# A hybrid decoder block with 32 experts: weights of the first pair loaded by halves, weights of the last pair by units of 4 MB

## The chip, the cores and the metric

The kernel runs on one core of one Trainium2 chip. The metric is the device time of the kernel in microseconds. The time before is the median of three runs, 1120.93 us (1120.08 to 1121.37). All arithmetic on weights is in float32 or in pairs of a rounded high part and a low part.

## The reference

One layer of a decoder for 256 tokens of width 1024: a normalization, one projection of 5632 columns, an attention with 8 heads, a gated recurrence with 4 heads, and their merging by sigmoid gates; then, with `x` the residual stream,

```python
x = x + mixed @ w_out[l]                      # 1024 x 1024
h2 = rmsnorm(x, norm2_w[l])
logits = h2 @ router_w                        # 32 experts
top_v, top_e = lax.top_k(logits, 4)           # softmax over the four
gu = xb @ w_gate_up[e] + b_gate_up[e]         # 1024 x 2048 for each expert
glu = gate * sigmoid(1.702 * gate)            # gate, up clamped at 7
y = ((up + 1.0) * glu) @ w_down[e] + b_down[e]  # 1024 x 1024
x = x + (sum of the four weighted y)
```

and a last normalization. All 32 experts are computed, so 32 x 12 MB of expert weights are read from HBM.

## The kernel before

**The expert weights.** Experts are taken in pairs, 16 in all. The weights of a pair are 24 MB in 12 slots of 2 MB (128 partitions of 16 KB): slots 0 to 3 are gate/up of the pair's first expert, 4 to 7 those of the second, 8 and 9 the output weights (`w_down`) of the first, 10 and 11 those of the second. Two neighbouring slots are a unit of 4 MB. The ring in SBUF has just 12 slots (`slots`), so slot m of the next pair is loaded over slot m of this one once TensorE has used it. All these loads are issued by SyncE, in order, on one DMA queue. `load` (L475) loads a slot, `load_unit` (L479) a unit in one DMA. `load_pair` (L543) issues a pair's loads: where `by_slots` (L443) holds, each slot waits for its own release (`used`, L534) and is a DMA of its own; elsewhere both slots of a unit are waited for and one DMA of 4 MB follows. Before, `by_slots` holds for pairs 0, 1 and the last one (15). Slots 10 and 11 of the last pair are loaded in five parts (`parts`, L567, issued at L572): 1, 1, 1, 0.5 and 0.5 MB, each with a semaphore.

**What TensorE does with a pair.** `pair` runs gate/up of the first expert (slots 0 to 3, 16 matmuls a slot, L1817), then `combine` of the pair before (L1785), transpositions of the activation (`act_T`, L1863), gate/up of the second expert (slots 4 to 7), the output matmuls of the first (slots 8, 9, L1880), the gathering for the next pair (L1765) and the output matmuls of the second (slots 10, 11). In the last pair, the combinations of pair 14 lie between its slots instead, and a transposition of the second expert's activation lies between slots 8 and 9. After the last slot the result is combined once more (L1976), normalized and stored. Before each slot `arrived` (L1790) waits: for an even slot on `slot_loaded[m]`, for an odd one only if it was loaded on its own.

**Before the experts.** The dense weights come through a ring of three raw buffers. ScalarE rounds a piece of a weight to its high part (`round_hi`, L677) in a buffer `hi_a` to `hi_d`, and VectorE puts the low part over the raw data (`form_lo`, L464). `PIECES` (L38 on) says which half of which weight goes into which buffer. `hu`, `wo0` and `wo1` are the recurrence's up-projection and the two column halves of `w_out`. The slots of pair 0 lie over these buffers: slot 4 over the low parts of `hu`, 11 over its high parts (`hi_d`), 3 and 5 over high (`hi_a`) and low parts of `wo0`, 6 and 10 over those of `wo1`. So they can be loaded only once the matmuls that read them are through.

`mixed` (L1630) computes `wo0` for both token tiles (256 tokens are two tiles of 128). The high parts of `wo0` lie as two blocks of 256 columns with all 8 chunks of rows each, so every matmul reads both blocks, and both are needed until the end:

```python
for tt in range(TT):            # chunks 0 to 3: high, rest
turn_mix(3)
for tt in range(TT):            # chunks 4 to 7: high, rest
for tt in range(TT):            # chunks 0 to 7: low part of the input; end(...)
```

`wo1` is already handled in two halves of rows (chunks 0 to 3, 4 to 7), and `half_used` (L1732) marks that the first is done with.

SyncE issues the loads of pair 0 that lie over `hu`, `wo0` and `wo1` in this order: when `hu3` is full, slots 4 and 11; when `wo10` (the second tile of `wo0`) is full, slots 3 and 5; on `half_used`, the first halves of 6 and 10; when `wo11` is full, their second halves; last slot 9. Then pair 1 follows, its slot 0 in two halves (L550, L552).

Of the kernel before, what the change touches and what calls it, by code (L numbers as in the profile page):

```python
# [11 lines left out]
P = 128  # L12
# [3 lines left out]
KD = D // P  # L16
# [13 lines left out]
PAIRS = E // 2  # L30
# [23 lines left out]
    [(GA1, j, "dve", ("D", j), "kT1") for j in range(2)] + [(GB0, j, "dve", ("A", j), "ga1") for j in range(2)] + \  # L54
    [(GB1, j, "dve", ("D", j), "ga3") for j in range(2)] + \
    [("mu", j, "dve", ("QA", j), "gb1") for j in range(4)] + [("hu", j, "dve", ("QD", j), "gb3") for j in range(4)] + \
    [("wo0", j, "dve", ("A", j), "mu3") for j in range(2)] + [("wo1", j, "dve", ("KB", j), None) for j in range(2)]
AT_PIECE = {(p[0], p[1]): n for n, p in enumerate(PIECES)}


# [66 lines left out]
def hybrid_block(nc, A, out):  # L127
    ctx = ExitStack()
    with ctx:
# [186 lines left out]
        def hi_part(where):  # L316

            buf, j = where
            if buf == "KB":
                return hi_b[:, 2048 * j:2048 * j + 2048].rearrange("p (k n) -> p k n", k=4)  # L320
            if buf in ("QA", "QD"):
                return {"QA": hi_a, "QD": hi_d}[buf][:, 1024 * j:1024 * j + 1024].rearrange("p (k n) -> p k n", k=4)
            return {"A": hi_a, "B": hi_b, "C": hi_c, "D": hi_d}[buf][:, 2048 * j:2048 * j + 2048].rearrange(
                "p (k n) -> p k n", k=KD)
# [10 lines left out]
        def raw_part(what, j, lo=False):  # L335

            s, kn = LOADS.index(what) % RING, 4 if what in ("mu", "hu") else KD
            whole = w_lo[s].rearrange("p (k n) -> p k n", k=kn) if lo else (wr4 if kn == 4 else wr8)[s]
            return whole[:, 4 * j:4 * j + 4, :] if what == "wo1" else whole[:, :, 256 * j:256 * j + 256]


        PS = [ctx.enter_context(nc.psum_tensor(f"PS{b}", [P, 512], F32)) for b in range(BANKS)]
# [46 lines left out]
        first_loaded, cst_loaded, router_loaded = sem("first_loaded"), sem("cst_loaded"), sem("router_loaded")  # L389

        first_half_used = sem("first_half_used")
        x_free, half_used, half_loaded = sem("x_free"), sem("half_used"), sem("half_loaded")

        slot_loaded = [sem(f"slot_loaded{m}") for m in range(12)]
        part_loaded = [sem(f"part_loaded{n}") for n in range(3)]
# [46 lines left out]

        def by_slots(j, m, first_round):  # L443

            return not first_round or j < 2 or j == PAIRS - 1

        def odd_loads(m, first_round, pairs=PAIRS):

# [22 lines left out]
        def _(sp):  # L471
# [41 lines left out]
                    sp.dma_start(MSK, A["lmask"].rearrange("p (m t) -> p m t", t=CHUNK)).then_inc(lmask_loaded, 16)  # L513


            filled(sp, "hu3")
            load(0, 0, 4)
            load(0, 0, 11)
            filled(sp, "wo10")
            for m in (3, 5):  # L520
                load(0, 0, m)
            for part in range(2):
                if part:
                    filled(sp, "wo11")
                else:
                    sp.wait_ge(half_used, 1)
                c = slice(2048 * part, 2048 * part + 2048)
                for m in (6, 10):
                    sp.dma_start(slots(m)[:, c], slot_src(0, m)[:, c]).then_inc(slot_loaded[m] if part else half_loaded, 16)
            filled(sp, "lg1")  # L530
            sp.wait_ge(root2_ready, TT)
            load(0, 0, 9)
# [10 lines left out]
            def load_pair(p, e, j, first_round, stop=12):  # L543

                for m in range(0, stop, 2):
                    if by_slots(j, m, first_round):
                        for n in (m, m + 1):
                            if first_round and j == 1 and n == 0:
                                sp.wait_ge(first_half_used, 1)
                                sp.dma_start(slots(0)[:, 0:2048], slot_src(e, 0)[:, 0:2048]).then_inc(half_loaded, 16)  # L550
                                used(0, 0)
                                sp.dma_start(slots(0)[:, 2048:], slot_src(e, 0)[:, 2048:4096]).then_inc(slot_loaded[0], 16)  # L552
                                continue
                            used(p + (n - SLOTS) // 12, (n - SLOTS) % 12)
                            load(e, j, n)
                    else:
                        for n in (m, m + 1):
                            used(p + (n - SLOTS) // 12, (n - SLOTS) % 12)
                        load_unit(e, j, m)
# [826 lines left out]
        def _(pe):  # L1386
# [243 lines left out]
            def mixed():  # L1630

                ps = [claim("wo00"), claim("wo10")]
                n, s = AT_PIECE["wo0", 1], LOADS.index("wo0") % RING
                w_h = hi_a.rearrange("p (j k n) -> p k j n", j=2, k=KD)
                w_l = w_lo[s].rearrange("p (k n) -> p k n", k=KD)

                def high(tt, ks):
                    for k in ks:
                        mm(ps[tt][:].rearrange("p (j n) -> p j n", j=2), mix_hi[:, k, P * tt:P * tt + P], w_h[:, k],
                           start=(k == 0), stop=False)  # L1640

                def rest(tt, ks):
                    for k in ks:
                        mm(ps[tt][:], mix_hi[:, k, P * tt:P * tt + P], w_l[:, k, :], start=False, stop=False)

                pe.wait_ge(hi_ready, n + 1)
                for tt in range(TT):
                    pe.wait_ge(mix_hi_ready, tt + 1)
                    high(tt, range(4))
                    wait_lo("wo0", 1)  # L1650
                    rest(tt, range(4))
                turn_mix(3)
                for tt in range(TT):
                    pe.wait_ge(mix_hi_ready, tt + 3)
                    high(tt, range(4, 8))
                    rest(tt, range(4, 8))
                for tt in range(TT):
                    wait_drained(pe, f"mT{2 + tt}")
                    for k in range(KD):
                        ins = mm(ps[tt][:].rearrange("p (j n) -> p j n", j=2), mix_lo[k // 4][:, k % 4, P * tt:P * tt + P], w_h[:, k],  # L1660
                                 start=False, stop=(k == KD - 1))
                    end(ins, f"wo{tt}0")

            mixed()
            def keep_clock(free_bank, cols):
# [63 lines left out]
            claim("wo11")  # L1729
            high1(ps[1], 1, 0)  # L1730
            rest1(ps[1], 1, 0)
            low1(ps[1], 1, 0).then_inc(half_used, 1)  # L1732
            high1(ps[0], 0, 1)
            rest1(ps[0], 0, 1)
            end(low1(ps[0], 0, 1), "wo01")
# [54 lines left out]
            def arrived(at, m):  # L1790

                r, j = at
                slot = ring(j, m)
                if isinstance(r, int) and isinstance(j, int) and j == 0 and m in (6, 10):
                    pe.wait_ge(half_loaded, 32)
                if not isinstance(j, int) and m == 0:
                    pe.wait_ge(half_loaded, 48)
                if m % 2 == 0:
                    pe.wait_ge(slot_loaded[m], 16 * (j + 1) if isinstance(r, int) else r * (16 * PAIRS) + 16 * (j + 1))
                elif not isinstance(j, int):  # L1800
                    pe.wait_ge(slot_loaded[m], 32)
                elif isinstance(r, int):
                    if by_slots(j, m - 1, True):
                        pe.wait_ge(slot_loaded[m], 16 * odd_loads(m, True, j + 1))
                else:
                    pe.wait_ge(slot_loaded[m], r * (16 * PAIRS) + 16 * (odd_loads(m, True) - PAIRS + j + 1))
                return slot
# [219 lines left out]
```

## Time and profile before

| what | us |
| --- | --- |
| median of 3 runs | 1120.93 |
| the profiled execution, its own time | 1120.51 |
| its span, first to last instruction | 1118.7 |
| TensorE busy | 1081.1 (97%) |
| VectorE, ScalarE, GpSimd busy | 347.6, 223.1, 47.9 |
| DMA | 438.77 MB, 392 GB/s over the span |

The time lies some 1.8 us over the span. Times in the views are counted from the start of the span. In a timeline, a row merges neighbouring instructions of one kind: start, duration of the whole, engine (PE is TensorE, DVE VectorE, ACT ScalarE, SPq SyncE's queue), line, operation, tiles (output<-inputs) and count; brackets tell how long the engine stood still before and on what it waited. `M`, `W`, `PS` are the names of the buffers; all slots are parts of `W`.

### The profile page before, as it was taken

Reading aid. Unit: us, or ns where it says so; the run is one execution under the profiler, and the core shown is the slowest. Engines: PE = TensorE matmul, PEld = TensorE weight load, DVE = VectorE, ACT = ScalarE, POOL = GpSimd, SP = SyncE. Lnnn points to the kernel's source line nnn. Section 1 sums busy time; section 2 is a strip of 40 time slices with the busy share of each in tenths; the row PEclk is TensorE's granted clock in tenths of the full one; section 3 lists DMA queues with packets and bytes.
Section 4 is the critical chain, followed back from the end, with each engine's and each line's share of the span. In section 5 each row is a group of like instructions: output and inputs, shape, how many; then the busy total and the mean of one; then the engine's idle time right before and its main releaser. Section 6 shows DMA issues by size and latency. Waiting matters only on the chain.

```text
span 1118.7 us, 14793 instructions
## 1 busy us (share of the span) xinstructions
PE 1081.1 (97%) x6265; PEld 528.2 (47%) x6265; DVE 347.6 (31%) x685; ACT 223.1 (20%) x355; POOL 47.9 (4%) x38
## 2 busy tenths in 40 slices
PE   7999999999999999999999999899999999999997
PEld 7889888734343434343443434234343334343432
DVE  4994888422222130312222221030303030312212
ACT  6645774301010101010101010001010101010102
POOL 0392000000000000000000000000000000000000
PEclk9999999999999999999999999899999999999999
DMA  9547549999999999999999999999999999999996
GB/s 323 194 152 308 218 163 388 382 425 400 418 431 432 431 431 431 431 432 431 431 431 431 431 431 431 431 431 431 432 431 435 434 431 431 431 435 431 422 426 247
DMA packets 35625, 438.77 MB, mean 392 GB/s; under 512 B 2900, under 2 KB 5736, under 8 KB 20488
## 3 DMA queue, kind: packets, MB, share of 16 engines
q1 hardware_dynamic: 34672, 437.76, 93.2%
q10 hardware_dynamic: 920, 0.56, 0.2%
q8 instruction: 23, 0.38, 0.1%
q14 instruction: 10, 0.08, 0.0%
HBM read 437.25 MB, written 1.05 MB: 392 GB/s over the span
## 4 chain that ended last, share of the span: by engine, by line
PE 71%; DMA 17%; DVE 2%; issue 1%; another core or an unknown queue 1%; SPq 0%; ACT 0%; DVEq 0%
PE PS L1817 31%; PE PS L1880 16%; DMA W<-in_w_gate_up_dram 9%; DMA W<-in_w_down_dram 8%; PE PS L1765 4%; PE PS L1785 4%; PE PS L1863 2%; PE PS L1469 2%; PE PS L1473 2%; PE PS L1476 2%; PE PS L1839 1%; PE PS L1455 1%; PE PS L1900 1%; DVE w_lo L464 1%
## 5 line engine op out<-in xcount | busy, mean ns | idle before, releaser
L1817 PE MATMUL PS<-W,M 128*64 128x512 f32 x2048 | 458.0, 599 | 16.0 <-DMA W<-in_w_gate_up_dram 10.2
L1817 PEld LDWEIGHTS PS<-W,M 128*64 128x64 f32 x2048 | 142.6, 138 | 300.1 <-issue 280.8
L1880 PE MATMUL PS<-W,M 128*64 128x512 f32 x1024 | 226.5, 594 | 7.7 <-DMA W<-in_w_down_dram 7.6
L1288 DVE TENSOR_SCALAR M<-PS 128x256 f32<-128x256 f32 x64 | 27.0, 422 | 512.2 <-PE PS L1817 512.2
L1880 PEld LDWEIGHTS PS<-W,M 128*64 128x64 f32 x1024 | 73.7, 137 | 146.1 <-issue 141.4
L868 ACT ACTIVATE M<-M 128x256 f32<-128x256 f32 x64 | 26.7, 417 | 474.3 <-DVE M L1288 474.3
L873 ACT COPY M<-PS 64x512 f32<-64x512 f32 x31 | 17.9, 578 | 268.8 <-PE PS L1880 268.8
L1304 DVE COPY M<-PS 128x512 f32<-128x512 f32 x32 | 22.1, 691 | 131.6 <-PE PS L1863 131.6
L1765 PE MATMUL PS<-M,X 128*128 128x128 f32 x480 | 57.6, 278 | 0.0
L1785 PE MATMUL PS<-M,SELT 128*128 128x512 f32 x120 | 55.8, 606 | 0.0
L1765 PEld LDWEIGHTS PS<-M,X 128*128 128x128 f32 x480 | 54.7, 192 | 1.0
L638 POOL TENSOR_SCALAR W<-W,SMALL 128x512 f32<-128x512 f32 x1 | 1.9, 1854 | 1010.9 <-DVE SMALL L1371 1010.9
L1298 DVE TENSOR_TENSOR M<-M 128x256 f32<-128x256 f32 x64 | 38.6, 604 | 4.9 <-ACT M L868 2.7
L1785 PEld LDWEIGHTS PS<-M,SELT 128*128 128x128 f32 x120 | 21.5, 189 | 34.0 <-issue 34.0
L1863 PE MATMUL PS<-CST,M 64*64 64x64 f32 x1024 | 36.7, 221 | 0.0
L464 DVE TENSOR_TENSOR w_lo<-raw,hi_a 128x2048 fp32r<-128x2048 f32 (+1 forms) x16 | 32.5, 2054 | 11.3 <-ACT hi_a L677 11.3
L1863 PEld LDWEIGHTS PS<-CST,M 64*64 64x64 f32 x1024 | 32.3, 134 | 5.9 <-issue 2.4
L1280 DVE TENSOR_TENSOR M<-PS,SMALL 128x512 f32<-128x512 f32 x32 | 22.1, 692 | 33.9 <-PE PS L1765 32.6
L1473 PE MATMUL PS<-w_lo,hT_hi 128*128 128x512 f32 x128 | 31.7, 389 | 0.0
L1294 DVE SCALAR_TENSOR_TENSOR M<-M 128x256 f32<-128x256 f32 x64 | 27.2, 425 | 2.2
L677 ACT CAST hi_a<-raw 128x2048 fp32r<-128x2048 f32 (+1 forms) x16 | 26.6, 1694 | 4.3 <-DMA raw<-in_w_in_dram 2.6
L1292 DVE TENSOR_SCALAR M<-PS 128x256 f32<-128x256 f32 x64 | 26.4, 413 | 0.0
(267 smaller groups left out, 853.5 us busy)
## 6 DMA issues: line engine op xcount, KB each, us to landing
W<-in_w_gate_up_dram SPq DMA_DIRECT2D x52, 4096.0 KB, 41.3
W<-in_w_down_dram SPq DMA_DIRECT2D x26, 4096.0 KB, 44.0
W<-in_w_gate_up_dram SPq DMA_DIRECT2D x22, 2048.0 KB, 12.6
raw<-in_w_in_dram SPq DMA_DIRECT2D x10, 2048.0 KB, 8.7
W<-in_w_down_dram SPq DMA_DIRECT2D x9, 2048.0 KB, 12.7
W<-in_w_down_dram SPq DMA_DIRECT2D x5, 1024.0 KB, 45.8
raw<-in_w_out_dram SPq DMA_DIRECT2D x2, 2048.0 KB, 10.5
W<-in_w_gate_up_dram SPq DMA_DIRECT2D x4, 1024.0 KB, 8.0
```

What stands on the lines that cost most here:

```text
L464: tensor_tensor(raw_part(what, j, lo=True), raw_part(what, j), hi_part(PIECES[n][3]), ALU.subtract).then_inc(lo_ready[PIECES[n][2]], 1)
L677: st.did(nc.scalar.copy(hi_part(PIECES[n][3]), raw_part(what, j)), hi_ready)
L868: nc.scalar.activation(sg, gate[b], ACT.Sigmoid, scale=ALPHA).then_inc(sigm_ready, 1)
L1288: v.tensor_scalar(gate[b], g2[:, :, 0], LIMIT, None, ALU.min).then_inc(gate_ready, 1)
L1294: v.scalar_tensor_tensor(out=up[b], in0=up[b], scalar=1.0, in1=gate[b], op0=ALU.add, op1=ALU.mult).then_inc(up_ready, 1)
L1298: v.tensor_tensor(act[b].rearrange("p (c q) -> p q c", c=8)[:, 32 * half:32 * half + 32, :], up[b].rearrange("p (q c) -> p q c", c=8), sg. ...
L1473: mm(ps[:], hi[:, k, rows], w_l[:, k], start=False, stop=False)
L1765: ins = mm(dst[:, P * a:P * a + P], hidden(tt, 4 * part + a), sel[:, tt, :], start=(tt == 0), stop=(tt == TT - 1))
L1785: ins = mm(acc[tt][n][:], selT[:, P * tt:P * tt + P], Y[:, 512 * n:512 * n + 512], start=False, stop=True, skip_group_check=True)
L1817: ins = mm(gu[half][64 * g:64 * g + 64, :], hTe[:, k, tok], gu_slot[slot][:, kk, c:c + 512], start=(k == 0), stop=(k == KD - 1))
L1863: ins = mm((gu[1] if b else multi)[rows, cols], act[b][rows, cols], ident[rows, rows], start=True, stop=True)
L1880: ins = mm(dst[64 * n:64 * n + 64, :], actT[b][:, 4 * kh + k, :], dn_slot[slot][:, k, 512 * n:512 * n + 512], start=(kh == 0 and k == 0), ...
```

## The change

Five things change. `wo0`'s high parts are laid out by halves of rows in `hi_a` (piece name `KA`), and `mixed` goes through it by halves of rows. The first half of `wo0` gets a mark of its own (`half_used["wo0"]`). The first loads of slots 4, 11, 3 and 5 are issued by halves, each half as soon as its part of the buffer is free: `hu1`, `hu3`, `half_used["wo0"]`, `wo10`. Slot 4's halves are column halves, the others contiguous halves of a partition's row. In `arrived`, the six slots of pair 0 that come in halves wait for all six first halves together; the first half of slot 0 of pair 1 has a semaphore of its own. And in the last pair `by_slots` holds from slot 10 on only, so that its slots 0 to 9 come as five units of 4 MB.

```diff
@@ -54,7 +54,7 @@
     [(GA1, j, "dve", ("D", j), "kT1") for j in range(2)] + [(GB0, j, "dve", ("A", j), "ga1") for j in range(2)] + \
     [(GB1, j, "dve", ("D", j), "ga3") for j in range(2)] + \
     [("mu", j, "dve", ("QA", j), "gb1") for j in range(4)] + [("hu", j, "dve", ("QD", j), "gb3") for j in range(4)] + \
-    [("wo0", j, "dve", ("A", j), "mu3") for j in range(2)] + [("wo1", j, "dve", ("KB", j), None) for j in range(2)]
+    [("wo0", j, "dve", ("KA", j), "mu3") for j in range(2)] + [("wo1", j, "dve", ("KB", j), None) for j in range(2)]
 AT_PIECE = {(p[0], p[1]): n for n, p in enumerate(PIECES)}
 
 
@@ -316,8 +316,8 @@
         def hi_part(where):
 
             buf, j = where
-            if buf == "KB":
-                return hi_b[:, 2048 * j:2048 * j + 2048].rearrange("p (k n) -> p k n", k=4)
+            if buf in ("KA", "KB"):
+                return (hi_a if buf == "KA" else hi_b)[:, 2048 * j:2048 * j + 2048].rearrange("p (k n) -> p k n", k=4)
             if buf in ("QA", "QD"):
                 return {"QA": hi_a, "QD": hi_d}[buf][:, 1024 * j:1024 * j + 1024].rearrange("p (k n) -> p k n", k=4)
             return {"A": hi_a, "B": hi_b, "C": hi_c, "D": hi_d}[buf][:, 2048 * j:2048 * j + 2048].rearrange(
@@ -336,7 +336,7 @@
 
             s, kn = LOADS.index(what) % RING, 4 if what in ("mu", "hu") else KD
             whole = w_lo[s].rearrange("p (k n) -> p k n", k=kn) if lo else (wr4 if kn == 4 else wr8)[s]
-            return whole[:, 4 * j:4 * j + 4, :] if what == "wo1" else whole[:, :, 256 * j:256 * j + 256]
+            return whole[:, 4 * j:4 * j + 4, :] if what in ("wo0", "wo1") else whole[:, :, 256 * j:256 * j + 256]
 
 
         PS = [ctx.enter_context(nc.psum_tensor(f"PS{b}", [P, 512], F32)) for b in range(BANKS)]
@@ -442,7 +443,7 @@
 
         def by_slots(j, m, first_round):
 
-            return not first_round or j < 2 or j == PAIRS - 1
+            return not first_round or j < 2 or (j == PAIRS - 1 and m >= 10)
 
         def odd_loads(m, first_round, pairs=PAIRS):
 
@@ -513,20 +514,26 @@
                     sp.dma_start(MSK, A["lmask"].rearrange("p (m t) -> p m t", t=CHUNK)).then_inc(lmask_loaded, 16)
 
 
-            filled(sp, "hu3")
-            load(0, 0, 4)
-            load(0, 0, 11)
-            filled(sp, "wo10")
-            for m in (3, 5):
-                load(0, 0, m)
+            def load_half(m, part, across=False):
+
+                to, src = slots(m), slot_src(0, m)
+                if across:
+                    to, src = (a.rearrange("p (k n) -> p k n", k=4)[:, :, 512 * part:512 * part + 512] for a in (to, src))
+                else:
+                    to, src = (a[:, 2048 * part:2048 * part + 2048] for a in (to, src))
+                sp.dma_start(to, src).then_inc(slot_loaded[m] if part else half_loaded, 16)
+
             for part in range(2):
-                if part:
-                    filled(sp, "wo11")
-                else:
-                    sp.wait_ge(half_used, 1)
-                c = slice(2048 * part, 2048 * part + 2048)
-                for m in (6, 10):
-                    sp.dma_start(slots(m)[:, c], slot_src(0, m)[:, c]).then_inc(slot_loaded[m] if part else half_loaded, 16)
+                filled(sp, f"hu{2 * part + 1}")
+                load_half(4, part, across=True)
+                load_half(11, part)
+            for what, pair_of in (("wo0", (3, 5)), ("wo1", (6, 10))):
+                sp.wait_ge(half_used[what], 1)
+                for m in pair_of:
+                    load_half(m, 0)
+                filled(sp, "wo10" if what == "wo0" else "wo11")
+                for m in pair_of:
+                    load_half(m, 1)
             filled(sp, "lg1")
             sp.wait_ge(root2_ready, TT)
             load(0, 0, 9)
@@ -1630,36 +1637,36 @@
             def mixed():
 
                 ps = [claim("wo00"), claim("wo10")]
-                n, s = AT_PIECE["wo0", 1], LOADS.index("wo0") % RING
-                w_h = hi_a.rearrange("p (j k n) -> p k j n", j=2, k=KD)
-                w_l = w_lo[s].rearrange("p (k n) -> p k n", k=KD)
-
-                def high(tt, ks):
+                w_h = hi_a.rearrange("p (k n) -> p k n", k=KD)
+                w_l = w_lo[LOADS.index("wo0") % RING].rearrange("p (k n) -> p k n", k=KD)
+
+                def high_and_rest(tt, kh):
+                    pe.wait_ge(mix_hi_ready, 2 * kh + tt + 1)
+                    ks = range(4 * kh, 4 * kh + 4)
                     for k in ks:
-                        mm(ps[tt][:].rearrange("p (j n) -> p j n", j=2), mix_hi[:, k, P * tt:P * tt + P], w_h[:, k],
-                           start=(k == 0), stop=False)
-
-                def rest(tt, ks):
+                        mm(ps[tt][:], mix_hi[:, k, P * tt:P * tt + P], w_h[:, k], start=(k == 0), stop=False)
+                    wait_lo("wo0", kh)
                     for k in ks:
-                        mm(ps[tt][:], mix_hi[:, k, P * tt:P * tt + P], w_l[:, k, :], start=False, stop=False)
-
-                pe.wait_ge(hi_ready, n + 1)
+                        mm(ps[tt][:], mix_hi[:, k, P * tt:P * tt + P], w_l[:, k], start=False, stop=False)
+
+                def low(tt, kh):
+                    wait_drained(pe, f"mT{2 * kh + tt}")
+                    for k in range(4):
+                        ins = mm(ps[tt][:], mix_lo[kh][:, k, P * tt:P * tt + P], w_h[:, 4 * kh + k],
+                                 start=False, stop=(kh == 1 and k == 3))
+                    return ins
+
+                pe.wait_ge(hi_ready, AT_PIECE["wo0", 0] + 1)
                 for tt in range(TT):
-                    pe.wait_ge(mix_hi_ready, tt + 1)
-                    high(tt, range(4))
-                    wait_lo("wo0", 1)
-                    rest(tt, range(4))
+                    high_and_rest(tt, 0)
                 turn_mix(3)
+                low(0, 0)
+                low(1, 0).then_inc(half_used["wo0"], 1)
+                pe.wait_ge(hi_ready, AT_PIECE["wo0", 1] + 1)
                 for tt in range(TT):
-                    pe.wait_ge(mix_hi_ready, tt + 3)
-                    high(tt, range(4, 8))
-                    rest(tt, range(4, 8))
+                    high_and_rest(tt, 1)
                 for tt in range(TT):
-                    wait_drained(pe, f"mT{2 + tt}")
-                    for k in range(KD):
-                        ins = mm(ps[tt][:].rearrange("p (j n) -> p j n", j=2), mix_lo[k // 4][:, k % 4, P * tt:P * tt + P], w_h[:, k],
-                                 start=False, stop=(k == KD - 1))
-                    end(ins, f"wo{tt}0")
+                    end(low(tt, 1), f"wo{tt}0")
 
             mixed()
             def keep_clock(free_bank, cols):
@@ -1729,7 +1736,7 @@
             claim("wo11")
             high1(ps[1], 1, 0)
             rest1(ps[1], 1, 0)
-            low1(ps[1], 1, 0).then_inc(half_used, 1)
+            low1(ps[1], 1, 0).then_inc(half_used["wo1"], 1)
             high1(ps[0], 0, 1)
             rest1(ps[0], 0, 1)
             end(low1(ps[0], 0, 1), "wo01")
@@ -1791,10 +1798,10 @@
 
                 r, j = at
                 slot = ring(j, m)
-                if isinstance(r, int) and isinstance(j, int) and j == 0 and m in (6, 10):
-                    pe.wait_ge(half_loaded, 32)
+                if isinstance(r, int) and isinstance(j, int) and j == 0 and m in (3, 4, 5, 6, 10, 11):
+                    pe.wait_ge(half_loaded, 6 * 16)
                 if not isinstance(j, int) and m == 0:
-                    pe.wait_ge(half_loaded, 48)
+                    pe.wait_ge(first_half_loaded, 16)
                 if m % 2 == 0:
                     pe.wait_ge(slot_loaded[m], 16 * (j + 1) if isinstance(r, int) else r * (16 * PAIRS) + 16 * (j + 1))
                 elif not isinstance(j, int):
```

Beside it, the declarations of the semaphores are changed, and slot 0 of pair 1 counts on `first_half_loaded`.

## Rows read from the trace of the kernel before

**Rows 1.** The page: its head, and TensorE in part 1.

```profile
span 1118.7 us, 14793 instructions
...
PE 1081.1 (97%) x6265; PEld 528.2 (47%) x6265; DVE 347.6 (31%) x685; ACT 223.1 (20%) x355; POOL 47.9 (4%) x38
```

**Rows 2.** Busy time by stretches; last three columns: TensorE's clock, DMA share, GB/s.

```profile
183.00:224.00 41.00, 40.39 (x222) 31.42 (x222) 22.64 (x53) 13.67 (x25) 0.00 (x0) 1.00 0.93 373
...
300.00:660.00 360.00, 358.74 (x2045) 145.91 (x2043) 75.14 (x186) 38.28 (x67) 0.00 (x0) 1.00 1.00 431
660.00:1046.00 386.00, 366.80 (x2031) 146.38 (x2028) 78.73 (x200) 37.05 (x67) 0.00 (x0) 0.99 1.00 431
```

**Rows 3.** Timeline of TensorE, 891 to 1040 us.

```profile
891.65 5.20 PE L1817 MATMUL PS<-W,M 128*64 128x512 f32 x16 [2.55 <-DMA W<-in_w_gate_up_dram]
...
1008.26 3.65 PE L1817 MATMUL PS<-W,M 128*64 128x512 f32 x16 [2.54 <-DMA W<-in_w_gate_up_dram]
...
1037.49 2.79 PE L1880 MATMUL PS<-W,M 128*64 128x512 f32 x12 [1.54 <-DMA W<-in_w_down_dram]
```

**Rows 4.** Timeline of all engines, 192 to 230 us.

```profile
192.75 3.79 PE L1660 MATMUL PS<-hi_a,mix_lo 128*128 128x512 f32 x16
...
196.44 2.04 DVE L1184 TENSOR_TENSOR X<-PS,X 128x512 f32<-128x512 f32 x2
...
219.40 10.52 PE L1817 MATMUL PS<-W,M 128*64 128x512 f32 x48
```

**Rows 5.** SyncE's loads by `W`, one each: issue (184.3, 272.7, 283.0), then to landing.

```profile
L477 SPq DMA_DIRECT2D W<-in_w_gate_up_dram x1: 328/328/328, 184.3 to 184.3; - x1
DMA to landing us min/median/max: 7.3/7.3/7.3
...
L477 SPq DMA_DIRECT2D W<-in_w_down_dram x1: 328/328/328, 272.7 to 272.7; - x1
DMA to landing us min/median/max: 9.4/9.4/9.4
...
L481 SPq DMA_DIRECT2D W<-in_w_gate_up_dram x1: 328/328/328, 283.0 to 283.0; - x1
DMA to landing us min/median/max: 13.9/13.9/13.9
```

**Rows 6.** The page, part 6: DMA issues, KB each, median us to landing.

```profile
raw<-in_w_in_dram SPq DMA_DIRECT2D x10, 2048.0 KB, 8.7
```

**Rows 7.** As rows 5: last unit of pair 14; slots 6, 7, 9 of pair 15.

```profile
L481 SPq DMA_DIRECT2D W<-in_w_down_dram x1: 327/327/327, 998.5 to 998.5; - x1
DMA to landing us min/median/max: 48.6/48.6/48.6
...
L477 SPq DMA_DIRECT2D W<-in_w_gate_up_dram x1: 328/328/328, 1031.7 to 1031.7; - x1
DMA to landing us min/median/max: 49.6/49.6/49.6
...
L477 SPq DMA_DIRECT2D W<-in_w_gate_up_dram x1: 3192/3192/3192, 1036.0 to 1036.0; - x1
DMA to landing us min/median/max: 51.4/51.4/51.4
...
L477 SPq DMA_DIRECT2D W<-in_w_down_dram x1: 4225/4225/4225, 1045.9 to 1045.9; - x1
DMA to landing us min/median/max: 51.2/51.2/51.2
```

**Rows 8.** Timeline of TensorE, 1070 to 1110 us.

```profile
1076.45 10.52 PE L1817 MATMUL PS<-W,M 128*64 128x512 f32 x48
...
1092.32 3.65 PE L1880 MATMUL PS<-W,M 128*64 128x512 f32 x16 [1.10 <-DMA W<-in_w_down_dram]
...
1097.12 7.09 PE L1880 MATMUL PS<-W,M 128*64 128x512 f32 x32
1104.58 3.65 PE L1880 MATMUL PS<-W,M 128*64 128x512 f32 x16 [0.37 <-DMA W<-in_w_down_dram]
```

More of the change, by code:

```diff
@@ L391, in hybrid_block @@
         first_half_used = sem("first_half_used")
-        x_free, half_used, half_loaded = sem("x_free"), sem("half_used"), sem("half_loaded")
+        x_free, half_loaded, first_half_loaded = sem("x_free"), sem("half_loaded"), sem("first_half_loaded")
+        half_used = {"wo0": sem("half_used_wo0"), "wo1": sem("half_used_wo1")}
         slot_loaded = [sem(f"slot_loaded{m}") for m in range(12)]
@@ L549, in load_pair @@
                                 sp.wait_ge(first_half_used, 1)
-                                sp.dma_start(slots(0)[:, 0:2048], slot_src(e, 0)[:, 0:2048]).then_inc(half_loaded, 16)
+                                sp.dma_start(slots(0)[:, 0:2048], slot_src(e, 0)[:, 0:2048]).then_inc(first_half_loaded, 16)
                                 used(0, 0)
```

## Prediction

> **What bounds the kernel now.** I read the page's head first: TensorE is busy for 1081 of 1118.7 us [rows 1]. That alone would say "TensorE bound", so the second view is the table by stretches [rows 2]. From 300 us to 1046 us the DMA share is 1.00 and the rate stands at 431 GB/s, whatever TensorE does: in 300 to 660 TensorE is busy for 358.7 of 360 us, in 660 to 1046 only for 366.8 of 386 us. So the stream of expert weights is saturated all along; TensorE starts behind it (the ring is full when it starts), catches up until about 660, and then waits. The timeline of TensorE shows where: it stands still for 2.54 us in front of the second gate/up unit of a pair and for 1.54 us in front of the first output unit [rows 3]. Between those two lie three units of 4 MB in 1037.49 - 1008.26 = 29.2 us, 9.74 us a unit; 4.194 MB at 431 GB/s gives 9.73. The end of the kernel is therefore the end of the stream plus what TensorE still has to do after the last landings, and the change is to be read in three places: does the stream get ahead in front, does it keep that, and what does TensorE have left when the last large piece lands.
>
> **Front: wo0 by rows.** The new mixed() issues the same 48 matmuls of 512 columns in another order, so at the durations of now (16 in 3.79 us [rows 4]) nothing changes on TensorE. The first output tile is full 4 matmuls before the second instead of 8, so some 0.9 us later; its reader, the residual addition on VectorE, starts at 196.44 now, when VectorE is through with the low parts of wo1 [rows 4], and the first tile would be full at about 192.75 + 3.79 - 0.9 = 195.6. Cost 0, 0.8 us of cover. The casts and subtractions have the same number of elements; cost 0. SyncE now waits for hu1 and for two half_used marks; behind those waits stand only the loads of pair 0 that it issued later before. TensorE now waits for all six first halves before slot 3 of pair 0; they are issued during the w_out matmuls, at the moments of now or before, and slot 3 comes after the 48 matmuls that start at 219.4 and take 10.5 us [rows 4]: no cost.
>
> **Front: the twelve half loads.** Between 183 and 224 us the stream moved 373 GB/s instead of 431 [rows 2]: 41 x (1 - 373/431) = 5.5 us were lost, because slots 4/11, 3/5, 6/10 wait for matmuls. A 2 MB load on an empty queue lands 7.3 us after its issue (184.3), 2.4 us more than the 4.9 us that it takes in a full one [rows 5] (the 4.9 is worked out below); the halves fill most of such holes. The column halves of slot 4 have runs of 2 KB; the nearest loads, those of w_in with such runs, land in 8.7 us [rows 6], so at most 1.4 us per 2 MB goes back, in a stretch that has holes anyway: 0.
>
> But what is won has to get past the releases of pair 1. Those come from TensorE, which is dense there and is not moved. Slot 10 of pair 1 is issued at 272.7 and lands 9.4 us later, at 282.1; on an empty queue it would land at 272.7 + 7.3 = 280.0. Pair 2's first unit is issued at 283.0 and lands at 296.9; on an empty queue, 283.0 + 7.3 + 4.9 = 295.2 [rows 5]. So however early pair 0 is there, no more than 296.9 - 295.2 = 1.7 us passes this point. The other end is 0: with 9.4 us from issue to landing against 7.3 the queue is nearly drained there already, and the slowest of the 16 engines need not be the one that a hole lets catch up. I take 1.0 us, in between; both ends are kept.
>
> The Trainium skill (DMA: Bandwidth & Descriptors, section on the fixed cost) gives each DMA about 2.0 us of its own besides its bytes. On an empty queue the row agrees, with 2.4 us. In a full queue it does not hold, see the next part; by that rule five DMAs fewer would be 10 us.
>
> **Last pair: the gain of units.** The last unit of pair 14 lands at 998.5 + 48.6 = 1047.1, slot 6 of the last pair at 1031.7 + 49.6 = 1081.3 [rows 7]: 7 slots in 34.2 us, 4.89 us each, against 9.73 / 2 = 4.865. Ten slots as five units save 0.25 us. The landing of slot 7, at 1036.0 + 51.4 = 1087.4, came 1.2 us late (1081.3 + 4.9 = 1086.2). Nothing in the rows ties that to the size of the pieces, so it stays.
>
> **Last pair: what units take away.** In a unit TensorE can use slot m only when m+1 is there too. For the gate/up units this costs little: TensorE runs behind. Unit 6-7 would land at 1087.4 - 0.2 - 1.0 = 1086.2, and TensorE reaches slot 6 now at 1076.45 + 2/3 x 10.5 = 1083.5 [rows 8], so it waits some 2.7 us and is through with slot 7 at about 1094. Slots 8 and 9 are what matters. Now slot 8 lands at about 1092.2, is begun at 1092.32, and slot 9 lands during its work, at 1045.9 + 51.2 = 1097.1 [rows 7]; from there TensorE follows the parts and waits for the last slot's first part for only 0.37 us [rows 8]. After the change nothing of slots 8 to 11 can start before 1097.1 - 0.25 - 1.0 = 1095.85. What is then left on TensorE, without any wait, is 4.80 (slot 8 and the transposition, 1092.32 to 1097.12) + 7.09 (slots 9, 10) + 3.65 (slot 11) = 15.5 us [rows 8]. The parts of slots 10 and 11, 4 MB, are there 9.8 us after slot 9, at about 1105.7, when TensorE, begun at 1095.95, is still at slot 10: they are no longer late, TensorE is. End of the last matmul: 1095.85 + 0.1 + 15.5 = 1111.5, against 1104.58 + 3.65 = 1108.2 now. The work behind it does not change.
>
> **Sum.** 0 (mixed) - 1.0 (front) - 0.25 (fewer pieces) + 4.5 (TensorE's tail begins with slot 9's landing instead of slot 8's, 4.9 later, less the 0.37 us wait) = +3.3 us. The profiled execution took 1120.5 us with a span of 1118.7; it gives 1123.8. It lies 0.4 us under the median of the three runs shown, 1120.93; against that the change is +0.26%. About 0.2%, 2.2 us, is what a measurement of this kernel can tell from no change.
>
> **Rivals.**
> A, not slower: the whole front gain is carried. If the queue in 264 to 283 is not bound by the releases, but by something that an earlier start moves, 5.5 us get through instead of 1.0: 1123.8 - 4.5 = 1119.3, no change. It decides from 4.3 us on (then the tail is paid for). For it: the loss in 183 to 224 is real. Against it: the two issue times and TensorE's density. 0.13.
> B: the 1.2 us stall before slot 7 belongs to single slots and vanishes: 1122.6. For it: SyncE's issue of just that load took 3.19 us instead of 0.33 [rows 7]. 0.14.
> C: the clock falls. TensorE will stand still for some 2.7 and 1.8 us in the last pair. One stop of 2.55 us was followed by 16 matmuls in 5.20 us instead of 3.65, another of 2.54 us was not [rows 3]. Before slot 6 such a loss would vanish in the wait for unit 8-9; before slot 8 it adds 1.55: 1125.4. 0.08.
> D: each piece in the full queue has a price like that of a lone one (this is where the skill's fixed cost would lead): five fewer at 2.4 us bring the stream 12 us ahead, then TensorE alone bounds the last pair and only its two waits there, 1.47 us, and the 1.0 us in front come off: 1118.0, faster. Against it: 4.89 against 4.865. 0.03.
>
> **Chances and range.** My case has 0.62: 1123.8, by its bounds 1123.1 to 1124.8. Of it 0.50 lies above the 2.2 us line at 1123.2 and 0.12 within it. A: 0.11 same, 0.02 faster. B: 0.12 same, 0.02 slower. C: slower. D: faster. Together slower 0.60, same 0.35, faster 0.05. For the range: my bounds with B's taken off reach 1121.9, C reaches 1125.4; a part of A's way (some 3 us carried) gives 1121.8 and less. 1120.6 to 1125.4 leaves out D and most of A, under 2 in 10.
>
> **What would show it.** Front: the rate in 183 to 224 near 420, TensorE's first expert matmuls still at 219.4. Second unit of pair 2 and later landings 0 to 1.7 us earlier. Last pair: a wait of TensorE of some 2 to 3 us before slot 6 and of 1.5 to 2 us before slot 8, at about 1096; from there no wait on a DMA to the last expert matmul, 15.5 us later. I am wrong if slot 8 starts before 1093, if TensorE still waits for a part of slot 11, or if landings from 300 us on are 3 us earlier or more.

## The result and the profile after

The changed kernel takes 1124.24 us (median of 9 runs, 1123.31 to 1126.56), the kernel before, measured alongside, 1120.93 us (9 runs, 1120.08 to 1122.48). The ratio is 1.0036, 95% interval 1.0027 to 1.0045: slower by 0.36%, some 4 us by the ratio and 3.3 us between the medians, against the 3.3 us on 1120.5 that were forecast. The profiled execution took 1124.13 us, its span is 1122.3 us, 3.6 us longer than the one before.

First the page's head and TensorE's part, then the table by stretches (clock, DMA share and GB/s last):

```profile
span 1122.3 us, 14801 instructions
...
PE 1085.2 (97%) x6265; PEld 530.3 (47%) x6265; DVE 348.1 (31%) x685; ACT 223.2 (20%) x355; POOL 45.9 (4%) x38
```

```profile
183.00:224.00 41.00, 40.40 (x223) 31.68 (x223) 23.20 (x53) 14.22 (x25) 0.00 (x0) 1.00 0.98 381
300.00:660.00 360.00, 358.50 (x2043) 145.76 (x2041) 75.11 (x186) 38.30 (x67) 0.00 (x0) 1.00 1.00 432
660.00:1046.00 386.00, 370.20 (x2012) 146.91 (x2010) 78.71 (x199) 36.37 (x66) 0.00 (x0) 0.98 1.00 431
```

Nothing has changed in the long stretch: the stream runs at 431 to 432 GB/s from 300 us on. In front the rate rose only from 373 [rows 2] to 381 GB/s. What the halves won there shows best in the loads of SyncE. These are, of the changed kernel, the second half of slot 6 (209.8), slot 9 (213.7), pair 1's slot 10 (273.3), pair 2's first unit (283.6), pair 14's last unit (999.4) and, of the last pair, the units of slots 6-7 (1038.6) and 8-9 (1045.6), each with its time to landing:

```profile
L524 SPq DMA_DIRECT2D W<-in_w_gate_up_dram x1: 328/328/328, 209.8 to 209.8; - x1
DMA to landing us min/median/max: 6.9/6.9/6.9
...
L478 SPq DMA_DIRECT2D W<-in_w_down_dram x1: 328/328/328, 213.7 to 213.7; - x1
DMA to landing us min/median/max: 11.0/11.0/11.0
...
L478 SPq DMA_DIRECT2D W<-in_w_down_dram x1: 328/328/328, 273.3 to 273.3; - x1
DMA to landing us min/median/max: 9.0/9.0/9.0
...
L482 SPq DMA_DIRECT2D W<-in_w_gate_up_dram x1: 328/328/328, 283.6 to 283.6; - x1
DMA to landing us min/median/max: 14.7/14.7/14.7
...
L482 SPq DMA_DIRECT2D W<-in_w_down_dram x1: 327/327/327, 999.4 to 999.4; - x1
DMA to landing us min/median/max: 48.6/48.6/48.6
...
L482 SPq DMA_DIRECT2D W<-in_w_gate_up_dram x1: 327/327/327, 1038.6 to 1038.6; - x1
DMA to landing us min/median/max: 48.2/48.2/48.2
...
L482 SPq DMA_DIRECT2D W<-in_w_down_dram x1: 327/327/327, 1045.6 to 1045.6; - x1
DMA to landing us min/median/max: 51.0/51.0/51.0
```

The reader is to see three things. Slot 9 of pair 0 landed 12.8 us after its issue before, and does so after 11.0 us now: the stream arrives 1.8 us less behind. At pair 1's slot 10 the lead is down to 0.4 us (9.0 us to landing, 9.4 before [rows 5]), and then it is gone. Pair 2's first unit lands 14.7 us after its issue, where it was 13.9 [rows 5], but that is one late transfer of this execution; at the second unit the two kernels are level, before and then changed:

```profile
L481 SPq DMA_DIRECT2D W<-in_w_gate_up_dram x1: 328/328/328, 290.7 to 290.7; - x1
DMA to landing us min/median/max: 16.9/16.9/16.9
...
L482 SPq DMA_DIRECT2D W<-in_w_gate_up_dram x1: 328/328/328, 291.3 to 291.3; - x1
DMA to landing us min/median/max: 16.7/16.7/16.7
```

And the last unit of pair 14 lands at 1048.0, 0.9 us later than before (1047.1 [rows 7]). Of this some 0.6 us is the start of the execution (TensorE's first expert matmul stands at 219.97, at 219.40 before [rows 4]); the rest, 0.3 us, is the wrong way.

The last pair is as forecast. TensorE's timeline in the changed kernel, slots 6 to 11, to be laid beside [rows 8]:

```profile
1086.86 3.65 PE L1824 MATMUL PS<-W,M 128*64 128x512 f32 x16 [1.22 <-DMA W<-in_w_gate_up_dram]
...
1091.11 3.65 PE L1824 MATMUL PS<-W,M 128*64 128x512 f32 x16
1096.67 3.65 PE L1887 MATMUL PS<-W,M 128*64 128x512 f32 x16 [1.91 <-DMA W<-in_w_down_dram]
1100.26 1.15 PE L1870 MATMUL PS<-CST,M 64*64 64x64 f32 x32
1101.33 10.52 PE L1887 MATMUL PS<-W,M 128*64 128x512 f32 x48
1112.98 0.70 PE L1983 MATMUL PS<-M,SELT 128*128 128x512 f32 x1 [1.12 <-DVE M L1354]
```

TensorE waits for the unit of slots 6-7, waits again for that of 8-9 (landing 1045.6 + 51.0 = 1096.6), and from there to the last expert matmul at 1101.33 + 10.52 = 1111.85 it never waits on a transfer. The last expert matmul ended at 1108.2 before. This end has moved by 3.6 us, all of the difference between the spans.

### The profile page after: what moved, and what is told of

Same layout as the page of the kernel before. It is cut to its first block, busy times and chain, and to the rows that moved or that the text cites. A ratio compares the mean times of both kernels' runs of the same rounds, so it can differ in the third digit from the quotient of the medians.

```text
span 1122.3 us, 14801 instructions
## 1 busy us (share of the span) xinstructions
PE 1085.2 (97%) x6265; PEld 530.3 (47%) x6265; DVE 348.1 (31%) x685; ACT 223.2 (20%) x355; POOL 45.9 (4%) x38
## 4 chain that ended last, share of the span: by engine, by line
PE 70%; DMA 27%; DVE 2%; issue 0%; ACT 0%; another core or an unknown queue 0%; SPq 0%; DVEq 0%
PE PS L1824 28%; DMA W<-in_w_gate_up_dram 17%; PE PS L1887 14%; DMA W<-in_w_down_dram 9%; PE PS L1476 3%; PE PS L1772 3%; PE PS L1480 3%; PE PS L1483 3%; PE PS L1792 3%; PE PS L1462 3%; PE PS L1870 2%; PE PS L1846 1%; PE PS L1442 1%; DVE w_lo L465 1%; PE PS L1515 1%; PE PS L1907 1%
## 5 line engine op out<-in xcount | busy, mean ns | idle before, releaser
L1295 DVE TENSOR_SCALAR M<-PS 128x256 f32<-128x256 f32 x64 | 27.0, 422 | 518.7 <-PE PS L1824 518.7
L465 DVE TENSOR_TENSOR w_lo<-raw,hi_a 128x2048 fp32r<-128x2048 f32 (+1 forms) x16 | 33.1, 2091 | 11.2 <-ACT hi_a L684 11.2
L1480 PEld LDWEIGHTS PS<-w_lo,hT_hi 128*128 128x128 f32 x128 | 24.0, 188 | 5.1
## 6 DMA issues: line engine op xcount, KB each, us to landing
raw<-in_w_out_dram SPq DMA_DIRECT2D x2, 2048.0 KB, 10.4
```

The lines of the kernel that those rows point to most:

```text
L465: tensor_tensor(raw_part(what, j, lo=True), raw_part(what, j), hi_part(PIECES[n][3]), ALU.subtract).then_inc(lo_ready[PIECES[n][2]], 1)
L1480: mm(ps[:], hi[:, k, rows], w_l[:, k], start=False, stop=False)
```

## The experiments

Each run is compared with the kernel before on the same chip. The first four take the change apart.

**Only the front half.** The changed kernel, last pair by single slots:

```diff
-            return not first_round or j < 2 or (j == PAIRS - 1 and m >= 10)
+            return not first_round or j < 2 or j == PAIRS - 1
```

> The changed kernel with the last pair's slots 0 to 9 as single slots again, so only the front half of the change is left. Theory 1 (the releases of pair 1 take all the front gain back): no difference from the kernel before, 1120.9 within 0.7 us; the last unit of pair 14 lands at 1047.1 to 1048. Theory 2 (my prediction's term, 1.0 us carried): 1119.9. Theory 3 (all 5.5 us of the front carried, paid for somewhere else): 1115.4. If slot 7's landing comes 1.2 us late again, the stall goes with single slots; if not, it came by chance.

Measured: 1120.29 against 1120.22 us, ratio 0.9996 (0.9987 to 1.0004). The medians give no difference, as theory 1 says; the interval still holds the 1.0 us of theory 2 (0.09%), and excludes theory 3. In its trace the stream reads as in the changed kernel: 381 GB/s in 183 to 224 us, pair 2's first unit 14.8 us after its issue. Slot 7 of the last pair came without the 1.2 us stall, so that stall is not a property of single slots.

**Only the last pair's half.** The kernel before with the line above the other way round.

> The kernel before with the last pair's slots 0 to 9 as five units, so only the last pair's half of the change is made. Theory 1: all of the slowdown is here, 1124.2 within 0.7 us; slot 8 begins with a wait near 1096 and TensorE needs 15.2 us from there to the last expert matmul. Theory 2 (the front gives 1.0 us): 1125.2. If the front did harm instead, this is faster than the changed kernel.

Measured: 1124.25 against 1120.22 us, ratio 1.0026 (1.0017 to 1.0036). That is the changed kernel's time: the whole slowdown sits in the units of the last pair. From slot 8 on TensorE takes 15.2 us here too; slot 8 begins at 1098.27. The profiled execution (1125.73 us) started its experts 1.4 us later than that of the kernel before (at 220.85 us), and two units came late in it (10.4 us after the one before instead of 9.7).

**Only slots 0 to 7 as units** (`m >= 8` in place of `m >= 10`).

> The changed kernel with slots 8 and 9 of the last pair as single slots; slots 0 to 7 stay units. Theory 1 (all of the cost is the unit of slots 8 and 9, and the units of gate/up save the 1.2 us stall and 0.3 us): 1119.5, faster than the kernel before by 1.4 us. Rival (the stall is independent of the piece size and comes back): 1120.7. Rival (the waits of TensorE before slots 2 and 6, made by units, are what costs): as slow as the changed kernel, 1124.

Measured: 1122.75 against 1120.22 us, ratio 1.0016 (1.0006 to 1.0027). A miss: slower than before, though slots 8 and 9 come singly. Its TensorE in the last pair:

```profile
1087.65 3.65 PE L1824 MATMUL PS<-W,M 128*64 128x512 f32 x16 [1.29 <-DMA W<-in_w_gate_up_dram]
1091.24 0.73 PE L1846 MATMUL PS<-bias_parts,pick 128*128 128x512 f32 x2
1091.90 3.65 PE L1824 MATMUL PS<-W,M 128*64 128x512 f32 x16
1095.38 3.60 PE L1887 MATMUL PS<-W,M 128*64 128x512 f32 x16
1098.92 1.15 PE L1870 MATMUL PS<-CST,M 64*64 64x64 f32 x32
1100.00 10.52 PE L1887 MATMUL PS<-W,M 128*64 128x512 f32 x48
```

After the wait for the unit of slots 6-7 it never waits again: 1100.00 + 10.52 - 1087.65 = 22.9 us of work, while the stream needs only 4 x 4.9 = 19.6 us for the rest, after which 1.2 us of work are left. So this unit costs 22.9 - 20.8 = 2 us by itself. I had looked for the cost only in the last unit. The rule that covers both is: the end is the latest, over all pieces, of "landing of the piece + all TensorE work that could not start without it".

**Only slots 8 and 9 as a unit** (`m != 8`).

> The changed kernel with slots 0 to 7 of the last pair as single slots and only slots 8 and 9 as a unit. Theory 1: the whole cost of the unit, 4.2 us (TensorE's tail starts with slot 9), and none of the savings: 1125.2 with the stall of 1.2 us in the stream, 1124.2 without it. Rival (the waits before slots 2 and 6 cost): near the kernel before, 1121.

Measured: 1127.82 us (6 runs, 1124.79 to 1129.14) against 1120.22, ratio 1.0054 (1.0038 to 1.0070). It is the slowest of all, by more than the 4.2 us that were expected for the unit: 6.1 us by the ratio, 7.6 us between the medians. The profile, of the slowest of the six executions (1129.14 us), shows one reason. TensorE's timeline and its clock in the stretch behind the wait (third column from the right):

```profile
1099.96 5.38 PE L1887 MATMUL PS<-W,M 128*64 128x512 f32 x16 [6.14 <-DMA W<-in_w_down_dram]
1105.27 1.15 PE L1870 MATMUL PS<-CST,M 64*64 64x64 f32 x32
1106.35 10.52 PE L1887 MATMUL PS<-W,M 128*64 128x512 f32 x48
```

```profile
1100.00:1104.00 4.00, 4.00 (x12) 1.36 (x14) 0.00 (x0) 0.00 (x0) 0.00 (x0) 0.57 1.00 412
```

With slots 6 and 7 coming singly TensorE runs ahead and then stands still for 6.14 us in one piece; afterwards the clock is granted at the lower level and 16 matmuls take 5.38 us instead of 3.65. This is rival C of the prediction, 1.7 us, on the critical path. In this execution the last expert matmul ends at 1116.9, 8.6 us later than before: 2.4 us of it were there when pair 14's last unit landed (1049.5; this execution began its experts at 222.03 instead of 219.40), 0.3 us came from the stream in the last pair (two slots landed 0.8 and 0.7 us late, where before one had landed 1.2 us late), and 5.9 us are TensorE's tail, 4.2 and the 1.7 of the clock. Whether the clock fell in the other five executions is not shown. In the changed kernel the gate/up units split the wait in two, 1.22 and 1.91 us, and the clock stays up.

**Slots 0 to 5 as units**, 6 to 9 single (`m >= 6`), to test the rule that came out of the miss.

> The changed kernel with slots 6 to 9 of the last pair as single slots and only 0 to 5 as units. Reckoning behind the unit of 6 and 7: TensorE needs 22.9 us from its landing to the last expert matmul, the stream 19.7 + 1.2, so that unit costs 2.0 us alone. Behind the unit of 4 and 5: TensorE about 30.0 without waits, the stream 29.4 + 1.2 = 30.6, so it costs nothing. Theory (end = the latest of these sums): 1120.3, as the kernel before and as the run with the front half alone. Rival (every unit costs): 1121 or more.

Measured: 1120.66 against 1120.74 us, ratio 0.9998 (0.9988 to 1.0007). The rule holds within the interval, which still allows a cost of 0.8 us: units cost nothing that can be seen as long as the stream, not TensorE, has the longer way to the end. It is close to the edge: in the profile TensorE does not wait again after slots 2 and 3 (1069.0) and ends its last expert matmul at 1109.8, while the stream alone (last part at 1108.2, 1.2 us of work behind it) would have allowed 1109.4.

The other five ask why the front brings nothing.

**Slot 11 of pair 0 later.** The kernel before with

```diff
             filled(sp, "hu3")
             load(0, 0, 4)
+            filled(sp, "wo10")
             load(0, 0, 11)
-            filled(sp, "wo10")
```

> The kernel before with slot 11 of pair 0 issued together with slots 3 and 5 instead of with slot 4, some 12 us later. The stream then has 2 MB more to move behind the last hole, and slot 9 of pair 0 lands some 2.1 us later (228.1). Theory 1 (the stream arrives at pair 1's slot 10 and pair 2's first unit with little to spare, since both are bound by TensorE's releases): 0.5 to 2 us slower than before, so 1120.9 to 1122.3 against 1120.4. Rival (the front has several us to spare there): no difference.

Measured: 1121.95 against 1120.74 us, ratio 1.0013 (1.0004 to 1.0022): 1.2 us slower. The last unit of pair 14 lands at 1049.7 (1047.1 before; 1.0 us of it is the later start of this execution). Pair 2's first unit:

```profile
L481 SPq DMA_DIRECT2D W<-in_w_gate_up_dram x1: 328/328/328, 284.1 to 284.1; - x1
DMA to landing us min/median/max: 16.1/16.1/16.1
```

16.1 us from issue to landing instead of 13.9: now the queue is late, not the release. Pair 0's slot 9 landed 17.4 us after its issue instead of 12.8, so of a lateness of 4.6 us there 1.2 us reach the end. The kernel before stands at a knee: later loads cost a part of what they are late, earlier ones bring nothing.

**TensorE shortened, with and without halves.** In both kernels three of four correction matmuls of `wo1` are left out, 24 in all, so the low terms of `wo1` are only partly computed:

```diff
-                for k in range(4 * kh, 4 * kh + 4):
+                for k in (4 * kh + 3,):
                     mm(ps[:], mix_hi[:, k, P * tt:P * tt + P], w1_l[:, k], start=False, stop=False)
...
-                for k in range(4 * kh, 4 * kh + 4):
+                for k in (4 * kh + 3,):
                     ins = mm(ps[:], mix_lo[kh][:, k - 4 * kh, P * tt:P * tt + P], w1_h[:, k], start=False, stop=(k == KD - 1))
```

With halves, single slots in the last pair:

> The front half of the change (last pair by slots, as in the run that had only the front half), and of the correction products of wo1 (rest1 and low1) only one matmul in four: 24 of 32 matmuls of 0.226 us are left out, so part of wo1's low terms is not computed. TensorE begins the experts up to 5.4 us earlier. Theory 1 (the releases by TensorE bind the stream in pairs 1 and 2, and the halves make the stream able to follow): 4.5 to 5.4 us faster than the kernel before, 1115.5. Theory 2 (the halves carry nothing in any case): the same as the kernel before shortened alike.

Without halves (the kernel before):

> The kernel before with the same 24 matmuls of wo1's correction products left out, no halves for slots 4, 11, 3, 5. Theory 1: here the queue is busy with pair 0 until about 224, so the stream cannot follow TensorE all the way: 2 to 3 us faster than before, 1118, thus 2 to 3 us behind the shortened kernel with halves. Theory 2: as fast as that one.

Measured: 1114.89 us with halves (ratio 0.9948, 0.9935 to 0.9962), 1116.75 us without (0.9964, 0.9950 to 0.9977), against 1120.74; five runs each. TensorE's first expert matmul stands at 214.93 and 215.12. The first half slot of pair 1, then pair 2's first unit, with halves:

```profile
L557 SPq DMA_DIRECT2D W<-in_w_gate_up_dram x1: 327/327/327, 216.9 to 216.9; - x1
DMA to landing us min/median/max: 7.6/7.6/7.6
...
L482 SPq DMA_DIRECT2D W<-in_w_gate_up_dram x1: 328/328/328, 278.6 to 278.6; - x1
DMA to landing us min/median/max: 13.3/13.3/13.3
```

and the same two without:

```profile
L550 SPq DMA_DIRECT2D W<-in_w_gate_up_dram x1: 327/327/327, 217.1 to 217.1; - x1
DMA to landing us min/median/max: 11.5/11.5/11.5
...
L481 SPq DMA_DIRECT2D W<-in_w_gate_up_dram x1: 327/327/327, 278.8 to 278.8; - x1
DMA to landing us min/median/max: 15.8/15.8/15.8
```

With TensorE 4.6 us earlier (the start of the executions taken off) the halves do carry: 7.6 against 11.5 us to landing at the start of pair 1, 13.3 against 15.8 at pair 2, and 1.9 us between the medians (the two intervals overlap a little). Theory 1 was right in kind; the kernel without halves gained 4.0 us, more than the 2 to 3 expected. So the front loads were not what held the stream in the kernel as it is: TensorE's releases were.

**Earlier releases without leaving anything out.** In pair 0 TensorE stands still for 1.74 us because VectorE forms two selectors between the first and the second gate/up accumulator. Pair 0 is taken out of VectorE's loop and they are formed afterwards:

```diff
-                if not last:
+                late = isinstance(p, int) and p == 0
+                if not last and not late:
                     select_weighted(e)
                     select(e + 2)
                 activate(p * 2, 0, 1)
+                if late:
+                    select_weighted(e)
+                    select(e + 2)
...
-            with ve.Fori(0, E // 2 - 1) as p:
+            pair(0, 0)
+            with ve.Fori(1, E // 2 - 1) as p:
```

On the kernel with the front half and single slots in the last pair:

> The front half of the change with single slots in the last pair, and in pair 0 VectorE empties the second gate/up accumulator before it forms the two selectors instead of after them. TensorE stands still 1.74 us for that in pair 0. Theory 1 (releases by TensorE bind the stream from pair 1's slot 10 on, and the halves let the stream follow): TensorE and the releases behind it are 1.6 us earlier, so 1.2 to 1.7 us faster than the kernel before, 1119.0. Rival (the lag of the slowest engine of the stream is what counts in pair 1): no difference from 1120.3.

On the kernel before:

> The kernel before with the same move of the selectors in pair 0 behind the second accumulator, without halves. Theory 1: the releases come 1.6 us earlier, but the queue is busy with pair 0 until 226 and reaches slot 10 of pair 1 only with the lag of now; 0.3 to 1.2 us faster than before, less than with halves. Rival: no difference.

Measured: 1118.73 us with halves (ratio 0.9985, 0.9977 to 0.9994), 1118.99 us without (0.9990, 0.9981 to 0.9999), against 1120.38. Both beat the kernel before (the second only just) and the changed kernel. The wait is gone; TensorE's timeline in pair 0 of the version with halves has the second expert's first two slots in one piece:

```profile
231.60 7.31 PE L1829 MATMUL PS<-W,M 128*64 128x512 f32 x32
238.84 1.12 PE L1905 MATMUL PS<-M,SELT 32*128 32x512 f32 x2
```

1.65 us for a wait of 1.74 us in the first of 16 pairs, although TensorE stands still for 17 us on transfers later on: a release that comes earlier at the start moves the whole stream. Whether the halves add anything to it these runs don't tell (0.3 us between the medians, inside both intervals).

All profiles together show how a lead gets lost, when times are counted from TensorE's first expert matmul:

| kernel | slot 9 of pair 0 lands | second unit of pair 2 lands |
| --- | --- | --- |
| before | 6.6 us | 88.2 us |
| changed | 4.8 | 88.0 |
| front half alone | 5.3 | 88.2 |
| slots 8 and 9 alone as a unit | 0.8 | 88.7 |
| slot 11 later | 11.2 | 89.6 |
| shortened, without halves | 11.0 | 89.2 |
| shortened, with halves | 7.1 | 87.3 |
| early release, with halves | 3.4 | 86.9 |
| early release, without | 6.8 | 85.1 |

In the first four the releases stand at the same distance from TensorE's start, and so does the second unit of pair 2, within 0.7 us, wherever between 0.8 and 6.6 us pair 0 ended. Being 4.6 us later costs 1.4 us there. The last row is one execution of 1117.43 us, out of a range of 1117.2 to 1121.3 us; that it gains 3.1 us there for releases that came 1.65 us earlier is not explained.

## Why the prediction was right, and where not

The time (1123.8 forecast, 1124.24 measured), the sign and the place were right. Point by point:

- **What bounds the kernel**: right. The last pair's landings and TensorE's way from there set the end in every run.
- **mixed(), 0 us**: nothing speaks against it. TensorE's idle time in 183 to 224 us is 0.60 us in the changed kernel, 0.61 before, and the first expert matmul moved with the start of the execution.
- **Front, 1.0 us, bounds 0 and 1.7**: nothing of it is seen. The run with the front half alone is 0.1 us slower at the medians and 0.4 us faster by its ratio, with an interval that holds everything from a loss of 0.4 to a gain of 1.5 us. The traces put pair 2's second unit at the same place behind TensorE's start (88.2 us before, 88.0 and 88.2 with the halves). Rival A, the full 5.5 us, is excluded. It was also priced wrongly: the loss in 183 to 224 us was not all to be had, because the holes wandered. With the halves the second half of slot 6 meets a nearly empty queue at 209.8 (6.9 us to landing, 8.3 for its twin of before), and slot 9 was only 1.8 us nearer. The forecast of "near 420 GB/s" in this stretch failed too: 381.
- **Fewer pieces, 0.25 us**: the five units of the profile land in 1096.6 - 1048.0 = 48.6 us, 9.7 each, which fits 9.73. In the row before, 50.0 us stood for the same bytes; 1.2 of that was the stall.
- **The 1.2 us stall stays**: wrong for the profiled execution, where it did not come. But rival B's reason is wrong as well. The stall was absent with single slots too, while two stalls of 0.7 us came in the run that had only the units. Nor is SyncE's long issue a sign of it: with the front half alone the issue of slot 9 took 8.0 us, and the slot landed 4.9 us after the one before.
- **TensorE's tail, 4.5 us**: right in kind, 0.3 us too large. From the landing of slots 8-9 to the last expert matmul it took 15.3 us against 15.6 forecast, since in one piece slots 9 to 11 take 10.52 us, not 7.09 + 3.65 = 10.74, and slot 8 with the transposition takes 4.66 us, not 4.80, which held a short gap. Before, 11.1 us lay between the landing of slot 9 and the same end. 15.3 - 11.1 = 4.2.
- **The waits before slots 2 and 6 are free**: true only beside the unit of slots 8-9. The run with slots 0 to 7 as units shows that the unit of 6-7 costs 2 us alone. Here the step asked how far TensorE ran behind at that moment, and not how much work it would have left.

The sum for the profiled execution, in its own terms: 0.9 (landing of pair 14's last unit, of it 0.6 from the start) - 1.4 (no stall, larger pieces) + 4.2 (tail) = 3.7, measured 3.6. That the total came out so near is in part luck, since two errors cancelled: the front's 1.0 us did not come, nor did the stall's 1.2 us. The clock (rival C) did not fall on the critical path in the changed kernel's profile, but did with slots 8 and 9 alone as a unit. Rival D (a price for each piece in a full queue) is refuted: five pieces fewer brought the stream forward by 0.2 us, not by 12.

The Trainium skill (DMA: Bandwidth & Descriptors, section on why a DMA increments its semaphore by 16) says that only the full count, after all engines' shares, means that the data has landed. The traces agree: slot 8 was begun 0.1 us after the landing of its own piece before and 0.1 us after that of the whole unit now, 4.4 us later (1092.32 and 1096.67).

## What to carry to other kernels

When a stream and an engine are both nearly saturated, size the last pieces backwards from the end: a piece may be large as long as the engine's whole work behind its landing is shorter than what the stream still has to bring. Here that allowed units up to slot 5 and forbade them from slot 6 on. And before loads are issued earlier, look whether the next loads wait for the queue or for a release; at the knee a load that is late costs a part of its lateness, and one that is early pays nothing.

## What the runs showed of the hardware

Stalls of the stream that belong to no load: transfers of one size follow one another within 0.02 us for hundreds of microseconds, and then a single one comes 0.2 to 1.5 us late. Between 230 and 310 us this happened in most of the profiles, and often to the same load (slot 9 of pair 1, 1.5 us late before, 0.9 in the changed kernel, 1.5 with the front half alone); in the last pair the places differed. The DMA records also hold fetches of instructions (16 KB each, about 1.0 us). One, at 1070.6 us, came before the late slot 7 of the kernel before, but no run changed them, so the cause of the stalls stays open.

The times from one execution to the next scatter over 4 us (the kernel before: 1119.1 to 1123.5 us in 29 runs), which is why every comparison above needed its interval. A part of that is there before the experts: in the profiles of the kernels whose dense part is as long as before, the first expert matmul stood between 219.4 and 222.0 us.

The clock after a short stop was not a matter of the stop alone. This is TensorE's timeline of the changed kernel in pair 14 and its table of the same stretch and of the last pair's:

```profile
1009.16 5.35 PE L1824 MATMUL PS<-W,M 128*64 128x512 f32 x16 [2.55 <-DMA W<-in_w_gate_up_dram]
```

```profile
1009.00:1012.00 3.00, 2.84 (x8) 0.96 (x10) 0.00 (x0) 0.00 (x0) 0.00 (x0) 0.54 0.89 382
1096.00:1100.00 4.00, 3.33 (x16) 1.26 (x16) 0.62 (x2) 0.00 (x0) 0.00 (x0) 1.00 1.01 422
```

The same stop of 2.54 us in the same pair left the clock up before (3.65 us for the 16 matmuls [rows 3]), and now it fell to the lower level, at a price of 1.7 us that the next wait swallowed. Over all the profiles stops of 2.5 to 2.6 us were followed now by 3.65 us for 16 matmuls, now by 5.1 to 5.4, and so were two stops of 2.0 us (3.65 with the last pair's half alone, 5.35 in the shortened kernel without halves). A plan that leaves such a stop in front of critical work should count with either.
